# Softmax weights of two attention branches applied on GpSimd ahead of the turning, in place of turned factors

## What is computed

```python
# branch 1 (SLC, selected blocks) and 2 (WIN, window) of the NSA mixer, branch 3 is DSA (top-k)
p   = masked_softmax(q @ k.T * scale - slope * dist, valid)   # one row of scores for each token
o   = p @ v
g   = sigmoid(gates)                                          # per token, head and branch
o_b = g[..., 0] * o_cmp + g[..., 1] * o_slc + g[..., 2] * o_win
o_a = o_dsa                                                   # DSA has no gate of its own
merged = sigmoid(gate_a) * (o_a @ w_up_a) + sigmoid(gate_b) * (o_b @ w_up_b)
```

## Time and profile before

| what | value |
|---|---|
| median of 3 runs | 742.16 us (742.0 to 742.4) |
| the profiled execution: time, span in the profile | 741.73 us, 740.0 us |
| busy: TensorE, VectorE, ScalarE, GpSimd | 731.7, 585.3, 437.7, 177.1 us |
| mean granted TensorE clock | 1.00 of full speed |

### The profile page before, as it was taken

One profiled execution on the slowest core, in us unless ns is written; L12 is line 12 of the kernel. 1 busy time (PEld: TensorE's weight loads), 2 busy tenths in 40 slices (PEclk: granted clock), 3 DMA queues, 4 the chain that ended last, 5 costly groups with the idle time before them and its releaser, 6 DMA issues.

```text
span 740.0 us, 12690 instructions
## 1 busy us (share of the span) xinstructions
PE 731.7 (99%) x4686; PEld 651.4 (88%) x4686; DVE 585.3 (79%) x1079; ACT 437.7 (59%) x803; POOL 177.1 (24%) x192
## 2 busy tenths in 40 slices
PE   9999999999999999999999999999999999999998
PEld 9998977877997778777888899999999888799997
DVE  5478889769986877666767988988887788897987
ACT  7768377756767897555356555566556544533341
POOL 3110336523555545300012422222220000000000
PEclk9999999999999999999999999999999999999999
DMA  9621221111111111102533333333332332323332
GB/s 336 252 81 50 76 87 58 57 29 58 53 54 47 49 58 58 57 31 85 199 115 96 105 114 105 96 97 104 114 115 86 100 100 86 108 92 114 115 123 77
DMA packets 22861, 71.00 MB, mean 96 GB/s; under 512 B 2448, under 2 KB 5648, under 8 KB 22544
## 3 DMA queue, kind: packets, MB, share of 16 engines
q1 hardware_dynamic: 22800, 70.19, 30.5%
HBM read 68.08 MB, written 2.10 MB: 95 GB/s over the span
## 4 chain that ended last, share of the span: by engine, by line
PE 83%; DVE 8%; ACT 5%; issue 2%; DMA 1%; POOL 0%; DVEq 0%; SPq 0%; POOLq 0%
PE psum L2143 23%; PE psum L2145 22%; PE psum L2144 22%; PE psum L2151 5%; PE psum L2340 4%; PE psum L2317 2%; PE psum L2318 2%; DVE w_lo L1481 1%; DMA x2T<-in_xT 1%; ACT w_hi L1056 1%; DVE prob L1695 1%; ACT h L1056 1%; ACT q_st L1056 1%; DVE x2T L1848 1%; PE psum L2158 1%
## 5 line engine op out<-in xcount | busy, mean ns | idle before, releaser
L1056 ACT ACTIVATE w_hi<-stage 128x512 fp32r<-128x512 f32 (+4 forms) x149 | 114.7, 777 | 30.6 <-PE psum L2145 26.8
L2143 PE MATMUL psum<-hT_hi,w_hi 128*128 128x256 f32 (+1 forms) x324 | 113.5, 350 | 0.8 <-DVE q_st L1637 0.6
L2144 PE MATMUL psum<-hT_lo,w_hi 128*128 128x256 f32 (+1 forms) x324 | 107.3, 331 | 0.0
L2145 PE MATMUL psum<-hT_hi,w_lo 128*128 128x512 f32 (+1 forms) x264 | 90.6, 343 | 0.0
L1481 DVE TENSOR_TENSOR w_lo<-stage,w_hi 128x1024 fp32r<-128x1024 f32 (+4 forms) x58 | 56.8, 985 | 41.3 <-ACT w_hi L1056 37.1
L1056 ACT ACTIVATE w_hi<-s_sum 128x1024 fp32r<-128x1024 f32 x46 | 48.7, 1060 | 54.3 <-PE psum L2145 52.0
L2144 PE MATMUL psum<-a_lo,w_hi 128*128 128x512 f32 (+1 forms) x224 | 77.0, 344 | 0.0
L1243 ACT ACTIVATE prob<-prob,neg_max 128x128 f32<-128x128 f32 (+3 forms) x96 | 53.8, 560 | 35.4 <-DVE neg_max L1695 34.7
L1020 POOL TENSOR_TENSOR w_lo<-stage,w_hi 128x512 fp32r<-128x512 f32 x46 | 59.6, 1300 | 36.2 <-ACT w_hi L1056 36.0
L2143 PE MATMUL psum<-t_hi,w_hi 128*128 128x256 f32 x240 | 67.9, 283 | 0.0
L2144 PE MATMUL psum<-t_lo,w_hi 128*128 128x256 f32 x240 | 67.9, 283 | 0.0
(11 more groups left out here) (316 smaller groups left out, 2042.4 us busy)
## 6 DMA issues: line engine op xcount, KB each, us to landing
stage<-in_panels SPq DMA_DIRECT2D x104, 512.0 KB, 3.6
xT_in<-in_xT SPq DMA_DIRECT2D x8, 260.0 KB, 5.1
x_in<-in_x SPq DMA_DIRECT2D x4, 512.0 KB, 7.3
phi<-in_phi SPq DMA_DIRECT2D x2, 1024.0 KB, 6.8
x2T<-in_xT SPq DMA_DIRECT2D x1, 2048.0 KB, 9.0
stage<-in_panels SPq DMA_DIRECT2D x8, 212.0 KB, 5.1
stage<-in_panels SPq DMA_DIRECT2D x4, 408.0 KB, 3.1
stage<-in_panels SPq DMA_DIRECT2D x4, 384.0 KB, 5.0
```

What stands on the lines that cost most here:

```text
L1056: return nc.scalar.activation(dst, src, ACT.Copy, scale=scale)
L2143: mm(dst, a_h, b_h, start=start, stop=False)
L2144: mm(dst, a_h, b_l, start=False, stop=False)
L2145: return mm(dst, a_l, b_h, start=False, stop=stop)
```

## The change

For WIN and DSA (`WEIGHED = WIN`, so branches 1 and 2 of 0 to 2) the factor is no longer turned. A new step `weigh` stands in every even step u from 34 to 96, for the pair of units u-2 and u-1, between `qk u` and `pT u-3`: VectorE waits for the exponential of unit u-1, takes the reciprocal of two row sums and (WIN) multiplies by the two gates; GpSimd waits for that and multiplies the two units' probabilities in place by their factor; TensorE's `pT` of these units now waits for GpSimd instead of ScalarE. `inv`, `fac` and the factor's multiplication go for the 8 tiles of WIN and DSA; DSA's `close` goes altogether and `o_a` with it: `oT_hi` and `oT_low` read the PSUM bank, and `oT_low` frees it. `OA_PLACES` changes. `FILL` and the rest of the order are as before.

```diff
@@ -99,7 +99,7 @@
 CMP_AT = 20
 QA_PLACES = 52, 53, 55, 56, 60, 62, 64, 68
-OB_PLACES, OA_PLACES = (70, 80, 81, 82), (85, 95, 96)
+OB_PLACES, OA_PLACES = (70, 80, 81, 82), (85, 88, 93)
 WARM = 8
 PLAIN = 2
@@ -160,6 +160,7 @@
     SLC, WIN, DSA = range(3)
+    WEIGHED = WIN
     units = [(br, tt, h) for br in (SLC, WIN, DSA) for tt in range(TT) for h in range(H)]
     NU = len(units)
     T_LAG, PV_LAG = 3, 4
@@ -210,8 +211,9 @@
     for ti in range(NU // H):
-        at_unit(ti * H + 9, "inv", ti, at=early)
-        at_unit(ti * H + 10, "fac", ti)
+        if ti // TT < WEIGHED:
+            at_unit(ti * H + 9, "inv", ti, at=early)
+            at_unit(ti * H + 10, "fac", ti)
     for tt in range(TT):
         s0 = tt * H + CMP_AT
         at_unit(s0, "cmpS", tt)
@@ -270,11 +272,13 @@
         ready = len(half_split)
         if u < NU:
             step("qk", u)
+        if 2 <= u <= NU and u % 2 == 0 and units[u - 1][0] >= WEIGHED:
+            step("weigh", u - 2)
         if 0 <= u - T_LAG < NU:
             step("pT", u - T_LAG)
         if u < NU:
             step("exp", u)
-        if u >= TAKEN_AT and (u - TAKEN_AT) % H == 0:
+        if u >= TAKEN_AT and (u - TAKEN_AT) % H == 0 and (u - TAKEN_AT) // H < DSA * TT:
             step("close", (u - TAKEN_AT) // H)
         for what in early.pop(u, []):
             step(*what)
@@ -300,7 +304,6 @@
             elif n % 2:
                 step("pv", n - 1)
                 step("pv", n)
-    step("close", NU // H - 1)
     step("oT_hi", 0, TT - 1)
     step("oT_low", 0, TT - 1)
     step("sigmoid", 0)
@@ -549,7 +552,6 @@
         square = place("square", [P, TT * H * DH], Z + 100 * K)
         square_late = place("square_late", [P, S], Z + 65 * K)
         relu = place("relu", [P, RELUS, S], Z + 59 * K)
-        o_a = place("o_a", [P, 2, 4, P], Z + 43 * K)
         cmp_e = place("cmp_e", [P, TT, H, CP], Z + 47 * K)
         cmp_pT = place("cmp_pT", [P, KH, S], Z + 51 * K)
         phi1 = [place(f"phi1_{i}", [P, CMP_LEN // 2, HID], Z + at * K) for i, at in ((0, 67), (1, 24))]
@@ -639,6 +641,8 @@
         exp_done = sem("exp_done")
         pv_done = sem("pv_done")
         inv_done = sem("inv_done")
+        pair_inv = sem("pair_inv")
+        weighed = sem("weighed")
         fac_spread = sem("fac_spread")
         oT_hi_done = sem("oT_hi_done")
         oT_lo_done = sem("oT_lo_done")
@@ -840,9 +844,12 @@
             return slice((k // 2 + k % 2 * KT // 2) * P, (k // 2 + k % 2 * KT // 2 + 1) * P)
-        def out_tile(m, tt):
-
-            return (o_b[:, tt, :, :], tt) if m else (o_a[:, tt % 2, :, :], TT + tt)
+        def out_tile(eng, m, tt):
+
+            if m:
+                return o_b[:, tt, :, :], tt
+            ps = wait_full(eng, ("O", DSA * TT + tt))
+            return ps.rearrange("p (k t) -> p k t", k=4), TT + tt
         def gate_order(t):
             _, m, i = tiles[t][:3]
@@ -881,7 +888,8 @@
                 sp.dma_start(phi1[i][:, :, :], phi1_w[i].rearrange("p (j h) -> p j h", h=HID)).then_inc(phi1_loaded, 16)
             for p in range(8, OUT0 + SLOTS):
                 load_panel(p)
-            sp.wait_ge(oT_lo_done, 2 * TT)
+            for tt in (TT - 2, TT - 1):
+                wait_drained(sp, ("O", DSA * TT + tt))
             sp.dma_start(x2T[:, :, :], xT[:, 0:S].rearrange("(k p) t -> p k t", p=P)).then_inc(x_reloaded, 16)
             for p in range(OUT0 + SLOTS, len(panels)):
                 load_panel(p)
@@ -1013,6 +1021,14 @@
                     else:
                         nc.gpsimd.tensor_tensor(dst, inv, gates[:, tt, :, 1 + br, None].to_broadcast([P, H, DH]),
                                                 ALU.mult).then_inc(fac_spread, 1)
+                elif kind == "weigh":
+                    u0, = a
+                    w = (units[u0][1] + 1) * P
+                    pool.wait_ge(pair_inv, (u0 - WEIGHED * TT * H) // 2 + 1)
+                    for u in (u0, u0 + 1):
+                        prob = probs[u % PROBS][:, 0:w]
+                        nc.gpsimd.tensor_tensor(prob, prob, row_inv[:, u:u + 1].to_broadcast([P, w]), ALU.mult)\
+                            .then_inc(weighed, 1)
                 elif kind == "split" and a[0] in pool_panels:
                     p, part = a
                     cols, _ = panel_part(p, part)
@@ -1265,15 +1281,15 @@
                     drain_tok(("cmpPT", a[0]), cmp_pT, a[0])
                 elif kind == "oT_hi":
                     m, tt = a
-                    src, n = out_tile(m, tt)
+                    src, n = out_tile(se, m, tt)
                     if m:
                         wait_full(se, ("O", 2 * TT - 1))
                         wait_drained(se, ("cmpO", tt))
+                        wait_drained(se, ("O", TT + tt))
                     else:
                         se.wait_ge(oT_lo_done, TT)
-                    wait_drained(se, ("O", TT * (1 if m else 2) + tt))
                     copy(oT_hi[m][:, :, tt * P:(tt + 1) * P], src).then_inc(oT_hi_done, 1)
                 elif kind == "kc_sq":
                     wait_drained(se, ("kc",))
@@ -1780,6 +1796,16 @@
                     ins = tt_op(o_b[:, tt, :, :], o_b[:, tt, :, :], ps, ALU.add)
                     drained(ins, ("cmpO", tt))
                     wait_drained(ve, ("cmpO", tt))
+                elif kind == "weigh":
+                    u, = a
+                    br, tt, h = units[u]
+                    ve.wait_ge(exp_done, u + 2)
+                    inv = row_inv[:, u:u + 2]
+                    if br == WIN:
+                        link(nc.vector.reciprocal(inv, row_sum[:, u:u + 2]))
+                        tt_op(inv, inv, gates[:, tt, h:h + 2, 1 + WIN], ALU.mult).then_inc(pair_inv, 1)
+                    else:
+                        nc.vector.reciprocal(inv, row_sum[:, u:u + 2]).then_inc(pair_inv, 1)
                 elif kind == "inv":
                     ti, = a
                     ve.wait_ge(exp_done, (ti + 1) * H)
@@ -1788,26 +1814,28 @@
                 elif kind == "close":
                     ti, = a
                     br, tt, _ = units[ti * H]
-                    wait_drained(ve, ("fac", ti))
+                    if br < WEIGHED:
+                        wait_drained(ve, ("fac", ti))
                     ps = wait_full(ve, ("O", ti)).rearrange("p (k t) -> p k t", k=4)
                     if br == WIN:
-                        link(tt_op(ps, ps, fac[:, :, :], ALU.mult))
+                        if br < WEIGHED:
+                            link(tt_op(ps, ps, fac[:, :, :], ALU.mult))
                         o = o_b[:, tt, :, :]
                         ins = tt_op(o, o, ps, ALU.add)
                     else:
-                        o = out_tile(br != DSA, tt)[0]
-                        if br == DSA and tt >= 2:
-                            ve.wait_ge(oT_lo_done, TT + tt - 1)
-                        ins = tt_op(o, ps, fac[:, :, :], ALU.mult)
+                        ins = tt_op(o_b[:, tt, :, :], ps, fac[:, :, :], ALU.mult)
                     drained(ins, ("O", ti))
                     wait_drained(ve, ("O", ti))
                 elif kind == "oT_low":
                     m, tt = a
-                    src, n = out_tile(m, tt)
+                    src, n = out_tile(ve, m, tt)
                     ve.wait_ge(oT_hi_done, n + 1)
                     tok = slice(tt * P, (tt + 1) * P)
-                    tt_op(oT_lo[m][:, :, tok], src, oT_hi[m][:, :, tok].bitcast(F32), ALU.subtract)\
-                        .then_inc(oT_lo_done, 1)
+                    ins = tt_op(oT_lo[m][:, :, tok], src, oT_hi[m][:, :, tok].bitcast(F32), ALU.subtract)
+                    if m:
+                        ins.then_inc(oT_lo_done, 1)
+                    else:
+                        drained(ins, ("O", DSA * TT + tt))
                 elif kind == "split" and a[0] not in pool_panels:
                     split_panel(*a)
                 elif kind == "mix":
@@ -2318,7 +2346,10 @@
                     full(mm(dst, q, k_lo, start=False, stop=True), ("S", s))
                 elif kind == "pT":
                     u, = a
-                    te.wait_ge(exp_done, u + 1)
+                    if units[u][0] >= WEIGHED:
+                        te.wait_ge(weighed, u - WEIGHED * TT * H + 1)
+                    else:
+                        te.wait_ge(exp_done, u + 1)
                     transposes(("PT", u), [probs[u % PROBS][:, j * P:(j + 1) * P] for j in range(units[u][1] + 1)])
                 elif kind == "pv":
                     n, = a
@@ -2399,7 +2430,11 @@
                     t, k = a
                     what, m, i, p, nk, c0 = tiles[t]
                     if what == "up" and i == 0 and k == 0:
-                        te.wait_ge(oT_lo_done, TT if m else 2 * TT)
+                        if m:
+                            te.wait_ge(oT_lo_done, TT)
+                        else:
+                            for tt in (TT - 2, TT - 1):
```

(1 more changed line is left out.)

## The result

The changed kernel takes 757.87 us (median of 5 runs, 756.67 to 758.61), the kernel before 742.16 us beside it (5 runs, 741.52 to 742.4): the ratio is 1.021, 95% interval 1.0197 to 1.0224. The forecast was 753 us, slower, within 745 to 763. The direction and the place are as forecast; the loss is 15.7 us where 11 was the forecast.

The account below looks back on a forecast made before the run. TensorE's in-order queue was taken to bound the kernel: 741.7 - 3.5 (transposes) - 0.3 (end) + 14.9 (stalls) = 752.8 us profiled, with the median of runs 0.4 above, so 753 us, within 745 to 763.

Parts of the forecast that it names:

- TensorE's queue is the bound: All through the attention: TensorE's in-order queue sets the time; matmuls removed are gained and waits added paid in full.
- The savings: On TensorE in WIN and DSA: eight groups of factor transposes go, 0.43 us each, 3.5 us in all.
- the end's 0.3: At the attention's end: without DSA's last close and factor a bank frees sooner, 0.3 us back, between 0 and 0.6.
- The multiplications: On GpSimd, weighing one unit's probabilities: 0.41, 0.62, 0.83 and 1.04 us for 128, 256, 384 and 512 columns.
- The stalls: At TensorE's turning in WIN and DSA: waits for GpSimd's weighted probabilities, 14.9 us in sum after corrections.
- the prediction's corrections: At late pairs: VectorE catching up -0.8, -0.6, -1.2; GpSimd's queue +1.5, +0.85, +0.4; shorter close -1.4 us.
- the fifteen late pairs: Of 32 pairs in WIN and DSA, 15 have weights ready after TensorE's turn, 0.03 to 3.05 us late, 16.2 us in all.
- third rival: On GpSimd and VectorE: shared SBUF interfaces draw operations out, some 3 us on VectorE; 761 us, chance 0.17 with more.
- Only the floor: At late pairs in WIN and DSA: only delays the order itself forces, 9.6 us over 13 pairs; 748 us, chance 0.22.
- Hidden: At TensorE's turning: GpSimd's multiplications cause no waits and only the savings remain; 738 us, chance 0.06.
- Contention: In WIN and DSA: slower GpSimd multiplications, drawn-out VectorE operations, no stall helping another; 761 us, chance 0.17 with more.
- Equal: In the attention: stalls are few because VectorE catches up and just pay for the transposes; 742 us, chance 0.05.

Follow-up runs that it names:

- Experiment 1: Changed kernel, but GpSimd multiplies a scratch tile and TensorE's turning waits only for the exponential; probabilities stay unweighted: 742.49 us, ratio 1.0009.
- experiment 6: Changed kernel with only DSA weighed by GpSimd, in pairs; WIN keeps its turned factors: 751.24 us, ratio 1.0121.
- experiment 3: Changed kernel with GpSimd multiplying a scratch tile, TensorE not waiting for it, and no reciprocals or gate products on VectorE for WIN and DSA: 741.31 us, ratio 0.9992.
- experiment 5: Changed kernel with each unit weighed by itself one step after its scores, instead of in pairs: 747.89 us, ratio 1.0078.
- experiment 9: Changed kernel with the filling of neighbouring steps exchanged in six places, to give TensorE work before late transposes: 762.3 us, ratio 1.0279.
- Experiment 8: Changed kernel with the turning of a unit four steps behind its scores instead of three, and a fifth probability buffer: 756.06 us, ratio 1.0195.

## Why the prediction came out as it did

**TensorE's queue is the bound, and a wait in it is paid in full.** Right: busy time hardly changed, the granted clock was 1.00, and the span grew by what the waits add up to. Experiment 1 gives about 15 us back by the wait alone. TensorE's busy time fell by 0.9 us and not by 3.5, as the prediction had it: overlapping matmuls are counted once, so the savings are read from starts.

**The savings.** Right in size: about 0.43 us at each of the eight factors, read off as jumps of -0.40 to -0.45 at units 40, 48, 64, 72 and 80 and hidden in the larger ones at 56 and 88. Not all of it was a gain. At 56 and 88 TensorE only came 0.43 us sooner to a stall, and at 42 too: there the reduction is 2.23 us later than before and TensorE 1.79. The prediction took off 3.5 and worked out the lateness at these places as if TensorE came at the old time, 1.3 us too little. Of the end's 0.3 (0 to 0.6), 0.43 came, and 0.83 was lost again at the MLP, for which I took nothing.

**The multiplications.** Right within 0.01 us at each width, from the line through the earlier trace rows. The Trainium skill ("GPSIMD Engine Reference", section 3.1) gives 4497 ns for 2048 columns of two full inputs; a quarter of that, an estimate, is 1.12, and 1.04 was measured for 512 columns with a spread factor, so the rows were the better guide.

**The stalls: the mis-sized term, 14.9 forecast and 17.9 measured.** Place by place, with the prediction's corrections put in:

```
unit       32   34   36   42   44   52   56   58   62   66   68   76   78   82   84   88   90   second units
forecast  0.0  1.0  0.0  0.6  0.8  0.7  1.2  0.4  0.2  1.5  0.75 0.7  1.95 1.2  1.15 1.1  1.35  0
measured  0.63 0.88 0.70 1.30 1.92 0.62 2.09 0.0  0.11 1.20 0.0  0.62 1.92 1.12 1.22 1.45 1.25  0.9
```

(56 and 88 with the 0.43 of a factor added back.) The forecasts add to 14.6, since the fifteen late pairs that the prediction lists add to 15.9 and not to its 16.2. In DSA the forecast is right to 0.1 us at five of eight places; 68 was counted and did not come, since VectorE caught up there (its reduction was 7.39 us later than before, TensorE 8.11); it came in experiment 6 (0.66), where WIN had its factors. Besides 78, the longest waits were not at 66, 84 and 90, as the prediction had them, but at 56 (1.93) and 44 (1.78).

In WIN the corrections failed: "where VectorE is behind through its own work, a stall already paid gives it time to catch up" took 0.8 from unit 36 and 0.6 from 44, and `close` being shorter took 0.7 more from 44. The trace shows 0.70 at 36 and 1.92 at 44. The step that failed is not the catching up but what came behind it, a delay that the prediction put at nothing. Before 44 VectorE starts on the compressed branch (`cmp_e`) 1.76 us later than before (206.43 against 204.67) where TensorE is 3.09 later, so it has made good the 1.3 us of the forecast. Then its next two operations, both with two inputs in SBUF, take 1.47 and 1.40 us instead of 1.12 and 0.42, and the 1.3 us are gone. GpSimd works beside them: its `w_lo` splits, which now stand behind a pair of multiplications:

```profile
205.90 1.19 POOL L1030 TENSOR_TENSOR prob<-prob,row_inv 128x256 f32<-128x256 f32 x2
207.04 2.73 POOL L1036 TENSOR_TENSOR w_lo<-stage,w_hi 128x512 fp32r<-128x512 f32 x2
...
207.15 1.47 DVE L1778 TENSOR_TENSOR cmp_e<-cmp_e,cmp_scale 128x256 f32<-128x256 f32 x1
208.66 1.40 DVE L1779 TENSOR_TENSOR cmp_e<-cmp_e,cmp_mask 128x256 f32<-128x256 f32 x1
```

Before, the same splits ran from 203.67 for 2.56 us, and the second of these operations was free of them (all four of its kind, before and after, ns min/median/max):

```profile
L1763 DVE TENSOR_TENSOR cmp_e<-cmp_e,cmp_mask x4: 424/426/426, 146.4 to 206.5; 128x256 f32<-128x256 f32 x4
L1779 DVE TENSOR_TENSOR cmp_e<-cmp_e,cmp_mask x4: 424/911/1402, 146.3 to 208.7; 128x256 f32<-128x256 f32 x4
```

At 36 it is the same: 0.65 us made good, 0.64 lost in these two operations (0.47 and 1.40 us instead of 0.80 and 0.43). At 56 the gate product of the pair takes 0.70 us instead of 0.16 beside GpSimd's gate tile, and at 32 it takes 0.49, with which `o_b` and the factor's transposes behind it come 0.63 late although no `weigh` is waited for; experiment 3 shows that this one goes when the small operations go.

Together the drawn-out operations are 2.8 us (0.64, 1.33, 0.54 and 0.33) of the gap between 14.6 and 17.9. The prediction had this as its third rival, at some 3 us, and left it out of the sum. Two smaller terms were missing too. At 42 GpSimd takes up the pair 0.45 us after its factors are ready, behind another operation in its queue. And a unit behind a stall turns 0.06 us later once more, fifteen times, 0.9 us in all, a size that I did not look for.

**The rivals.** "Only the floor", 748, is out: 44, 56 and 78 are longer than the order alone makes them. "Hidden", 738, is what experiment 1 was to give if nothing else had come in, and even there it is not reached. Contention is not the main cause: GpSimd's pairs were drawn out once in 32, and more distance alone takes 12.7 of the 14.2 us of waits away (experiment 5). But one of its parts, VectorE's drawn-out operations, is most of what the forecast lacked in WIN. (Its parts add to 762 and not to the prediction's 761.) "Equal" is out.

**What stays open.** That GpSimd draws VectorE's operations out is read from their lying beside each other; no run takes GpSimd's splits or its gate tile away. At units 39 and 54 experiment 3 shows the small operations as the cause. Unit 46 in experiment 1 (0.50), where the two `cmp_e` operations took 0.43 us each, I did not separate. Nor is it shown why the first product of the MLP comes 0.83 us later.

## What to carry to other kernels

In a written-out, in-order schedule a producer put onto an idle engine costs what its chain is longer than the distance: one step more of it took away 12.7 of 14.2 us of waits, a product cut to 0.20 us took 6.9. Count the work that the bound engine has between the producer's last input and the consumer's turn, and compare it with the whole chain (reduction, reciprocal, handovers, product). Small operations that this puts onto a third engine delay other chains that run through that engine at the time, and the work that waits behind the new producer in its engine's queue comes later and falls beside other operations, here VectorE's. So try such a change stage by stage and keep it only where the room is: here the last two tiles of twelve. Room made elsewhere, by a later consumer or moved filling, was taken from another wait each time.

## What the runs showed of the hardware

**TensorE's clock fell in or after a wait.** In experiment 9, around the wait of 3.69 us (columns as in the earlier trace rows; the clock is the number behind GpSimd's):

```profile
186.00:190.00 4.00, 4.00 (x36) 4.00 (x35) 1.44 (x6) 2.12 (x7) 3.01 (x4) 1.00 0.00 0
192.00:196.00 4.00, 0.83 (x4) 0.83 (x5) 3.64 (x17) 1.74 (x7) 1.74 (x3) 0.80 0.00 0
196.00:200.00 4.00, 4.00 (x21) 4.00 (x20) 1.31 (x4) 0.38 (x2) 1.01 (x1) 0.50 0.00 0
200.00:204.00 4.00, 4.00 (x32) 4.00 (x32) 2.63 (x10) 2.17 (x7) 0.95 (x3) 0.85 0.00 0
```

From 194.4, for 6.8 us, the granted clock is 0.50, the lower level (1.2 of 2.4 GHz). Matmuls that follow each other at 0.12 us before (190.13, 190.25, 190.37) do so at 0.21 (196.09, 196.30, 196.52). Two more such stretches of 3.4 us follow in that profile, from 218.3 in a wait of 3.44 us and from 255.8, 1.4 us after one of 1.92 us. Experiment 8 has one, from 272.4 to 275.8, behind a wait of 3.20 us:

```profile
268.00:272.00 4.00, 0.80 (x6) 0.36 (x6) 1.71 (x6) 3.98 (x9) 0.00 (x0) 1.00 0.44 131
272.00:276.00 4.00, 4.00 (x20) 2.66 (x17) 0.54 (x4) 2.15 (x5) 1.26 (x1) 0.57 0.00 0
```

In the changed kernel's profile, also with a wait of 1.93 us, it stayed at 1.00, so the length of the last wait alone does not tell it; in three of its five runs the mean clock was 0.995 to 0.998, and these took 757.9 to 758.6 us, 0.8 to 1.9 more than the two at 1.00. Whether the clock makes the difference between 757.87 and the profiled 756.67 is not shown, since none of the slower ones was profiled (0.995 took 757.91, 0.998 took 757.87 and 758.61).

**VectorE and GpSimd draw each other out.** Each of four operations of the compressed branch on VectorE (128x256, two inputs in SBUF) runs four times in each of the 14 traces. All 132 runs of one with no GpSimd operation beside them took 0.42 to 0.43 us; the 51 that took more than 0.50, up to 1.50, all lay beside one, and 41 lay beside one and took under 0.50. The operation `oT_low` of the changed kernel, with both inputs in SBUF and with one in PSUM (ns min/median/max):

```profile
L1834 DVE TENSOR_TENSOR oT_lo<-o_b,oT_hi x4: 1218/1464/1739, 281.0 to 304.9; 128x512 fp32r<-128x512 f32 x4
L1834 DVE TENSOR_TENSOR oT_lo<-psum,oT_hi x4: 678/684/692, 313.6 to 345.8; 128x512 fp32r<-128x512 f32 x4
```

In the kernel before, the same operation on `o_b` had a median of 0.687 us (0.642 to 1.286). One of the four, and the one pair of multiplications that took 2.06 us instead of 1.61, lie on each other:

```profile
302.68 2.06 POOL L1030 TENSOR_TENSOR prob<-prob,row_inv 128x384 f32<-128x384 f32 x2 [2.70 <-DVE row_inv L1808]
302.84 1.22 DVE L1834 TENSOR_TENSOR oT_lo<-o_b,oT_hi 128x512 fp32r<-128x512 f32 x1
```

This agrees with the Trainium skill ("GPSIMD Engine Reference", section 1, Specifications), that GpSimd's SBUF interfaces are shared with VectorE and contended by its instructions with two SBUF inputs. With GpSimd busy for 38.6 us more, the four `oT_low` on `o_b` took 5.9 us together instead of 3.3. At the fence's place this costs nothing, since TensorE turns the next unit (304.21) without a wait, and in its list of waits none is for `oT_lo`; at units 36, 44 and 56 it does cost.
